# A hybrid decoder step: sample state update in the dense stage, gating inside the scan, state-input weighting on VectorE

## What is computed

```python
# prompt: chunks of 128 tokens, H = 32 heads of 64, G = 4 groups, state size N = 128
decay = exp(where(causal, la_cs[i] - la_cs[j], -inf))
y_diag = einsum('bcijgr,bcjgrp->bcigrp', (C @ B) * decay, xdt)
chunk_states = einsum('bcjgn,bcjgrp->bcgrpn', B, xdt * decay_to_end)
y = y_diag + (C @ h_prev) * exp(la_cs)
# sample: one token from a carried state, 8 sequences
hs = exp(dt * a) * h0 + B * (x * dt)          # the new state is an output
ys = einsum('bgn,bgrpn->bgrp', C, hs)
# both
yg = (y + d_skip * x) * silu(z)
yg = yg * rsqrt(mean(yg * yg over a group) + eps) * gnorm_w
out = yg @ w_out
```

## Time and profile before

| | us |
|---|---|
| three runs, median (lowest to highest) | 1814.99 (1813.65 to 1815.94) |
| the profiled execution, its own time | 1813.57 |
| its span in the trace | 1811.5 |
| scan, first state update to last y_out | 144.8 to 291.0 |
| gating and group norm | 291.0 to 334.3 |
| out-projection | 334.3 to 377.5 |
| norm | 377.5 to 397.6 |
| dense feed-forward stage | 397.6 to 590 |
| layer 1 and final norm, not touched by the change | 590 to 1811 |

### The profile page before, as it was taken

One profiled execution on the slowest core, in us unless ns is written; L12 is line 12 of the kernel. 1 busy time (PEld: TensorE's weight loads), 2 busy tenths in 40 slices (PEclk: granted clock), 3 DMA queues, 4 the chain that ended last, 5 costly groups with the idle time before them and its releaser, 6 DMA issues.

```text
span 1811.5 us, 26186 instructions
## 1 busy us (share of the span) xinstructions
PE 1676.7 (93%) x9438; PEld 1435.7 (79%) x9438; DVE 1350.5 (75%) x1733; ACT 1094.9 (60%) x1093; POOL 227.9 (13%) x140
## 2 busy tenths in 40 slices
PE   5898884879999899979999999999999999999995
PEld 4887773869999898958888888888888888888883
DVE  5797788544444676468979878889789888888985
ACT  5555555334443463347767777677777777777774
POOL 1002211025444222300000000000000000000000
PEclk9988787989999999979999999999999999999997
DMA  6345563356647544439999999999999999999995
GB/s 180 117 144 152 165 169 96 106 162 187 172 135 205 187 150 130 144 131 374 356 362 386 352 379 372 357 385 364 349 394 353 372 379 354 377 370 351 392 356 186
DMA packets 246213, 482.38 MB, mean 266 GB/s; under 512 B 10659, under 2 KB 151203, under 8 KB 245835
## 3 DMA queue, kind: packets, MB, share of 16 engines
q1 hardware_dynamic: 233152, 448.00, 70.0%
q0 software_dynamic: 7152, 26.03, 5.3%
q10 hardware_dynamic: 5838, 7.41, 1.2%
HBM read 463.80 MB, written 17.80 MB: 266 GB/s over the span
## 4 chain that ended last, share of the span: by engine, by line
PE 85%; DVE 8%; ACT 3%; DMA 2%; issue 1%; DVEq 0%; SPq 0%; ACTq 0%; POOLq 0%
PE bank L1296 12%; PE bank L1298 12%; PE bank L1297 12%; PE bank L938 8%; PE bank L939 8%; PE bank L940 8%; PE bank L1318 6%; PE bank L1317 6%; PE bank L1319 6%; PE bank L1270 1%; ACT part L377 1%; DVE part L389 1%; PE bank L1084 1%; DVE arena L1405 1%; DVE rs L1343 1%
## 5 line engine op out<-in xcount | busy, mean ns | idle before, releaser
L1896 DVE TENSOR_TENSOR raw_r<-raw_w,part 128x2048 fp32r<-128x2048 f32 x336 | 759.4, 2290 | 129.9 <-ACT part L851 119.0
L851 ACT ACTIVATE part<-raw_w 128x2048 fp32r<-128x2048 f32 x336 | 636.6, 1917 | 164.6 <-DMA raw_w<-in_moe_w_gu_dram 118.3
L1296 PE MATMUL bank<-part,xh 128*128 128x512 f32 x896 | 358.3, 400 | 1.5 <-DVE xl L1851 1.5
L1298 PE MATMUL bank<-part,xl 128*128 128x512 f32 x896 | 354.3, 395 | 0.0
L1297 PE MATMUL bank<-raw_r,xh 128*128 128x512 f32 x896 | 354.3, 395 | 0.0
L938 PE MATMUL bank<-ah,part 128*128 128x264 f32 x928 | 278.5, 300 | 11.4 <-DVE al L1356 8.0
L940 PE MATMUL bank<-al,part 128*128 128x264 f32 x928 | 269.2, 290 | 0.0
L1296 PEld LDWEIGHTS bank<-part,xh 128*128 128x128 f32 x896 | 168.4, 188 | 41.3 <-issue 1.9
L1298 PEld LDWEIGHTS bank<-part,xl 128*128 128x128 f32 x896 | 168.3, 188 | 41.2
L389 DVE TENSOR_TENSOR raw_r<-raw_w,part 128x1536 fp32r<-128x1536 f32 (+2 forms) x65 | 120.7, 1859 | 106.2 <-ACT part L377 105.7
L1297 PEld LDWEIGHTS bank<-raw_r,xh 128*128 128x128 f32 x896 | 168.6, 188 | 39.2
(11 more groups left out here) (361 smaller groups left out, 2315.5 us busy)
## 6 DMA issues: line engine op xcount, KB each, us to landing
raw_w<-in_moe_w_gu_dram SPq DMA_DIRECT2D x227, 1024.0 KB, 5.6
raw_w<-in_moe_w_down_dram SPq DMA_DIRECT2D x112, 1024.0 KB, 5.0
raw_w<-in_ffn_w_gu_dram SPq DMA_DIRECT2D x44, 512.0 KB, 5.3
raw_w<-in_ssd_w_in_dram SPq DMA_DIRECT2D x20, 1024.0 KB, 5.2
raw_w<-in_sgu_w_in_dram SPq DMA_DIRECT2D x16, 1024.0 KB, 5.6
raw_w<-in_ffn_w_down_dram SPq DMA_DIRECT2D x16, 704.0 KB, 4.9
raw_w<-in_state_ssm_dram POOLq DMA_DIRECT2D x16, 512.0 KB, 5.9
out_dram<-raw_w POOLq DMA_DIRECT2D x16, 512.0 KB, 3.9
```

What stands on the lines that cost most here:

```text
L851: act.activation(first_half(ND + n, 0, SLOT), raw_w[:, q, :], ACT.Copy).then_inc(S("part1"), 1)
L1296: mm(out, xh[:, k, :], w[0][:, kk, c], start=(k == 0), stop=False)
L1298: ins = mm(out, xl[:, k, :], w[0][:, kk, c], start=False, stop=(k == DT - 1))
L1896: tt(second_half(ND + n, 0, SLOT), raw_w[:, q, :], first_half(ND + n, 0, SLOT).bitcast(F32), ALU.subtract).then_inc(S("part2"), 1)
```

## The change

**The sample's state.** The scan no longer updates the state. Since C·(decay x h + B x) = decay x (C·h) + x (C·B), step t reads the old state (the eight products with C), multiplies the sums by the decay and adds a term that is prepared once, from C·B of each sequence (`cb`, formed in the in-projection at n = 12). The new states are formed in the dense feed-forward stage: the old ones are loaded a second time into three buffers (`old`), ACT decays four of the eight parts per weight tile (`decayed`), DVE adds the input (`updated`), GpSimd's queue stores. B and C are broadcast to the partitions by DMA, through a small buffer in DRAM (`bc_d`), instead of PE and ACT. The state loads of the scan go from GpSimd's queue to SP's, among the weight loads.

**The gate.** z stays in PSUM; ACT forms tanh(z/2), `z_out` on DVE forms (tanh + 1) z, `gated` multiplies by y, ACT squares and PE sums in the scan, two steps behind. Root, reciprocal and scaling of groups 0 and 1 are done at steps 10 to 15, those of groups 2 and 3 behind the scan. `out_first` multiplies k = 0 to 7 of m = 0 and of m = 1 first, then the rest of both.

**The decays.** `log_decay` is now six matmuls in reduced precision, and one of them adds the causal mask, so that the exponential can be taken straight from PSUM with a bias; `segments` is gone.

**The weighting** of the chunk states' inputs goes from GpSimd to DVE. `split_2` is all on DVE. The conv rows are transposed behind m = 2 to 7 of the out-projection (`conv_rows`) and copied by `conv_out`; the norm behind waits for their stores.

The core of the diff:

```diff
-            for n in range(15):
-                split_2(pool, n, True)
...
-            weighted(0)
             for t in range(IT):
...
+                pool.wait_ge(S("upd"), 2 * t + 2)
+                pool.dma_start(h_out[t], old[t % TB]).then_inc(S(f"new{t % TB}"), 16)
+                if t in (3, 7):
+                    spread(drive[:, (t // 4) % 2], 0, t // 4 + 2, f"drive{(t // 4) % 2}")
+                if t + TB < IT:
+                    pool.wait_ge(S(f"new{t % TB}"), 16 * (t // TB + 1))
+                    state_again(t + TB)
```

ScalarE in the scan:

```diff
+                    act.activation(ce[:, t % 2], psum[7][:, 0:256].rearrange("p (h i) -> p h i", h=2), ACT.Exp).then_inc(S("el_ready"), 1)
...
+                    for h in range(2):
+                        for c in range(2):
+                            act.activation(ex[t % 2][:, 2 * h + c, :], psum[2 + t % 2][:, 256 * h + P * c:256 * h + P * c + P],
+                                           ACT.Exp, bias=nla[:, c, 2 * t + h:2 * t + h + 1]).then_inc(S("ex_ready"), 1)
...
+                    act.activation(th, psum[(CT + t - 1) % 2][:, 0:T], ACT.Tanh, scale=0.5).then_inc(S("th_ready"), 1)
...
+                if t >= 2:
+                    square(t - 2)
+                if t % 2 == 1 and t < IT - 1:
+                    split_1(act, 15 + t // 2)
+                if t == 10:
+                    act.wait_ge(S("gms_ready"), 2)
+                    act.activation(rs[:, :, :], rs[:, :, :], ACT.Sqrt).then_inc(S("groot_ready"), 1)
```

VectorE in the scan, and the new functions:

```diff
+            def z_out(u):
+
+                dve.wait_ge(S("th_ready"), u + 1)
+                stt(out=zT[:, u, :], in0=th, scalar=1.0, in1=psum[(CT + u) % 2][:, 0:T],
+                    op0=ALU.add, op1=ALU.mult).then_inc(S("z_ready"), 1)
+
+            def gated(u):
+
+                dve.wait_ge(S("z_ready"), u + 1)
+                dve.wait_ge(S("y_done"), u + 1)
+                tt(zT[:, u, :], zT[:, u, :], xbc[:, u, :], ALU.mult).then_inc(S("gated"), 1)
...
+                if t < IT:
+                    own.settle()
+                    step(tt(ys, ys, sdec[:, t, :], ALU.mult))
+                    own.did(tt(xbc[:, t, NP_:T], xbc[:, t, NP_:T], ys, ALU.add))
+                    own.settle()
+                    dve.nop().then_inc(S("y_sample"), 1)
                 if t % 2 == 1 and t < IT - 1:
                     split_2(dve, 15 + t // 2)
...
+                if t % 4 == 2 and g + 1 < G:
+                    weighted(g + 1)
```

TensorE's log decays, and the wait ahead of the norm:

```diff
+                    pe.wait_ge(S("ex_ready"), 4 * t - 4)
+                if t:
+                    pe.wait_ge(S("el_ready"), t)
...
+                mm(out[:, :], identr[:, :], maskr[:, :].unsqueeze(1).to_broadcast((P, 4, P)), start=True, stop=False)
...
+            residual(1, ahead_out)
+            conv_out(5)
+            dve.wait_ge(S("conv_out"), 80)
             norm(1, IT)
```

More of the change, by code:

```diff
@@ L46 @@
 SB = 3
-HB = 4
+TB = 3
 EPS = 1e-5
@@ L561, in _ @@
+            for k in range(TB):
+                pool.wait_ge(S(f"new{k}"), 16 * len(range(k, IT, TB)))
             pool.wait_ge(S("v_out"), 16)
+            pool.iota(ioti[:, :], pattern=[[1, P]], base=0, channel_multiplier=0).then_inc(S("consts"), 1)
             def gather():
@@ L767, in ahead_down @@
                 split_1(act, D0 + 2 * m + 3)
+                if m < 6:
+                    decayed(2 * m + 20)
+                    decayed(2 * m + 21)
+                if m == 7:
+                    for k in range(TB):
+                        act.wait_ge(S(f"new{k}"), 16 * len(range(k, IT, TB)))
+                    act.dma_start(wsr, i["sgu_w_s"][0].rearrange("g i j -> i g j")).then_inc(S("late_in"), 16)
+                    for k in range(2):
+                        act.dma_start(bsr[8 * k:8 * k + 8, :], i["sgu_b_s"][0]).then_inc(S("late_in"), 16)
             norm(2, IT, ahead_down)
@@ L1090, in _ @@
[L1090 to L1106 removed]
+                if t >= 2:
+                    group_square(t - 2)
@@ new lines, in out_first @@
+            def out_first():
+                pe.wait_ge(S("z_ready"), IT)
+                both = [None, None]
+                for m in range(2):
+                    both[m] = weight(20 + m)
+                    for k in range(8):
+                        pe.wait_ge(S("yg2"), k + 1)
+                        product(psum[m][:, 0:T], [u[:, k, :] for u in both[m]], (zh[:, k, :], zl[:, k, :]), k == 0, False)
+                    if m == 0:
+                        group_square(IT - 1)
+                for k in range(8, IT):
+                    pe.wait_ge(S("yg2"), k + 1)
+                    for m in range(2):
+                        ins = product(psum[m][:, 0:T], [u[:, k, :] for u in both[m]], (zh[:, k, :], zl[:, k, :]), False, k == IT - 1)
+                        if k == IT - 1:
+                            ins.then_inc(S("o_mm"), 1)
@@ L1114, in out_proj @@
                         pe.wait_ge(S("x_ready"), xbase + m - 1)
-                    for c in range(per):
+                    for c in range(per if n > 1 or m >= 2 else 0):
                         w = weight(n0 + per * m + c)
```

586 lines of the change are left out of this document (316 added, 270 removed).

## The result

The changed kernel takes 1786.87 us (median of four runs, 1781.87 to 1791.52) against 1815.3 for the kernel before, a ratio of 0.984 with an interval of 0.981 to 0.988. It is faster by 28 us. The forecast was 1771 with a range of 1752 to 1794: the sign and the range hold, the size doesn't; 44 us were expected. It is one of the slower runs of the changed kernel, which spread over 10 us; the four of the kernel before beside them spread over 2, those beside the experiments over 5 to 6.

What follows compares the result with a forecast made beforehand. The scan was taken as a loop through VectorE and ScalarE, with TensorE following. Gains 24 (scan), 31 (behind it) and 1.5, less 5.4, 5.4 and 2, gave 43.7 off 1813.6; with 1.4 for the median, 1771 us, range 1752 to 1794.

Steps and rivals of the forecast that it cites:

- T: End of the scan, at the last y_out: forecast 267 us against 291.0 before, 24 us gained, ends 255 and 280.
- The conv transposes: Out-projection, behind tiles m = 2 to 7: six groups at 0.9 us with hand-over, 5.4 us lost on TensorE.
- rival B: Dense feed-forward stage: state transfers delay the weights by 10 to 20 us, total 1779 to 1789; chance 0.10.
- Layer 1: Later stages: VectorE's splits alone in the memory without GpSimd's share, 1.5 us gained, bounds 0 to 3.
- rival A: Scan: the two loops interlock, hardly shortening it; 8.9 to 9.6 us a step, T 280 to 291, total 1784 to 1795; chance 0.16.
- wrong if steps stay near 9 us: Scan: sign that would refute the prediction, which expected 6.18 us a step and pairs of 12.4 on VectorE.
- loop start: Scan: loop begins near 137 us, after half a split, C·B product, sample prelude, split 14 and weighting 0 on VectorE.
- steps 0 and 1: Scan: backlog of splits and states, 9.1 us each, 18.2 together.
- steps 2 to 10, with the clock's allowance and the root: Scan: nine steps of 6.18 us plus two chunk states of 2.5, 60.6; 6 for the clock, 3 for the root.
- steps 11 to the end: Scan: five steps of 6.2 us plus reciprocal, scalings and second parts, 40.9, and 1.5 for the loop's end.
- TensorE's and ScalarE's loop: Scan: log_decay (0.7), y matmuls, z tile, a group sum, split_1, exponential and hand-overs; 12.2 us per pair of steps.
- rival D: Scan: broken work leaves TensorE at 1.2 GHz throughout, 11.5 us a step, T = 321, total 1825, slower; chance 0.06.

Runs made afterwards that it cites:

- experiment 7: Changed kernel with the wait for the stores of the last 1024 conv columns moved from ahead of the norm to behind it; 1785.30 us, ratio 0.984.
- experiment 1: Changed kernel with the scan's weight splits moved from the end of odd steps to the end of the next even step; 1771.41 us, ratio 0.977.
- experiment 2: Changed kernel with root and first parts one step later, behind the exponentials, and the mean square ahead of the weighting; 1768.90 us, ratio 0.974.
- experiment 4: Changed kernel with both the later weight splits and the moved normalization (root, first parts, mean square); 1757.28 us, ratio 0.968.
- experiment 8: Changed kernel with splits, normalization and conv-store wait moved, and mean squares at steps 6 and 10 ahead of y_out; 1750.74 us, ratio 0.966.
- experiment 3: Changed kernel with 14 unused matmuls of 248 columns added on TensorE behind the z tile of odd steps from 3 on; 1787.41 us, ratio 0.985.
- experiment 5: Changed kernel with the weighting of the chunk states' inputs back on GpSimd instead of VectorE; 1775.80 us, ratio 0.980.
- experiment 10: The kernel of experiment 8 with the weighting on GpSimd instead of VectorE; 1745.94 us, ratio 0.963.

## Why the prediction was right in sign and wrong in size

**What held.** Behind the scan: tile 2 begins at T + 18.0, or T + 18.7 from the last y_out, by which the prediction counts; 18 were forecast. The conv transposes lost 39.4 - 36.9 = 2.5 us on TensorE up to the end of m = 7, 5.4 were charged, and the norm lost 19.2 - 15.1 = 4.1 instead of 5.4; the DMA wait in it was 2.94 us against 3.0, and experiment 7 shows that 1.8 of them count. The residual of m = 1, by which the prediction put it, is not the mark: it stands at 315.85, as a split is ahead of it on VectorE, while TensorE goes on at 312.2. Dense stage: 203.6 against 203.5, so rival B did not come; the 2 us charged were not needed. The Trainium skill ("DMA: Bandwidth & Descriptors", section "Issuing engines are not separate DMA queues") has the transfers of all issuing engines interleave on the same 16 DMA engines. The trace agrees in that the weights' transfers landed later (8.4 us against 5.3 for a gate and up half), and the effect on the time was nothing, since they still landed ahead of need. Layer 1: 1.8 us gained, 1.5 estimated; no run shows whether for the reason given. The table loads at step 10 took 1.28 us each, as in the earlier trace rows, and from the end of the root to the next exponential are 1.31 us.

**What was luck.** The time lies above the forecast's own 1759 to 1784 and inside rival A's 1784 to 1795, to which 0.16 was given; the range holds it because it takes in A. The scan ended 27 us late, and some 6 came back because the norm, the conv transposes and the dense stage cost less than charged. The sign rests on the gain behind the scan.

**The step that failed is T**, 294.2 instead of 267: rival A's length in its place, and 3 us beyond its end. By the prediction's own sign ("wrong if steps stay near 9 us") its scan was wrong: steps 2 to 10 took 9.06 us on average, and pairs of them 15.9 to 20.2 instead of 12.4. Rival A had the loops interlock through y_out, settling and the bank of exponentials; experiments 1, 2 and 4 show that it was the splits, the first parts and the mean squares queued ahead of what releases TensorE. The working has T in four terms:

| term | forecast | measured | off by |
|---|---|---|---|
| loop start | 137 | 139.1 | + 2.1 |
| steps 0 and 1 | 18.2 | 17.3 | - 0.9 |
| steps 2 to 10, with the clock's allowance and the root | 60.6 + 6 + 3 | 81.5 | + 11.9 |
| steps 11 to the end | 40.9 + 1.5 | 56.3 | + 13.9 |

The 2.1 us at the loop start can't be told from chance: with the same code ahead of the loop it began at 139.1, 140.7 and 144.4. Two slips of the sums matter little: the seven terms of a step add up to 5.03, not 5.05, and half a pair of before is 8.97, not 9.1.

*Steps 2 to 10.* The shortest pair, 8 and 9, with the chunk states, took 15.87 us at a clock of 0.94 where 12.35 + 2.5 was summed. TensorE's and ScalarE's loop was sized 1 us too short per pair: log_decay takes 1.05 to 1.17 us at the full clock, not 0.7. Over the nine steps that makes 4.5, the mean squares 3.8 (see below); the 3.6 that are left are by this estimate the clock, beyond the 6 charged. The 6 were taken without a reason from a range that ended at 17; with the same waits the same code ran 8.5 us apart by its clock, and between the changed kernel and experiment 8 the same work differs by 21 us. Against rival D the prediction has TensorE's waits for y_out shrink. They did, but others took their place (29.3 us of waiting before, 32.1 after): VectorE and ScalarE were relieved, but the order in which they release TensorE was not. With another order the sum comes out: in experiment 8 steps 2 to 10 took 60.4 us and those behind 38.2, against the 60.6 and 42.4 of the working. So the work was sized well, and the order was not in the sum.

*Steps 11 on.* The normalization was summed as VectorE's work (3.6 + 8 x 0.43 + 8 x 0.36) with 3 for the root ahead of it. The work was right and the place was not: first parts stand ahead of the next exponential on ScalarE, and behind a split and the reciprocal on VectorE. A sum over one engine does not see a chain through three; experiment 2 moved the root, the first parts and the mean squares, and took out 12.6 us of waiting (3.8 of them the mean squares'), experiment 4 with the splits 20.2.

*The weighting.* It was charged as hidden under TensorE's chunk states. In fact the mean square was queued behind it on VectorE, and TensorE's next group sum behind that: 2.27 and 1.50 us, which the working does not have. The working asks what is queued behind an added wait, but not what is queued behind added work.

Rival D did not come: the scan's mean clock was 0.82, not 0.50. What sets how far it falls in one execution and not in the next stays open; the runs show only that less waiting goes with a higher clock (32 us of waits: 0.82 to 0.87; 27 to 18: 0.83 to 0.86; 12 to 9: 0.90 to 0.96), and that experiment 3, which put work into some of the gaps, does not settle whether the gaps are the cause.

## What to carry to other kernels

Relieving the fullest engine of a loop pays only as far as the next one allows: sum the loop for every engine, and where two come out alike, follow the order by which they release each other instead of taking the larger sum. In an in-order list the place of an instruction can cost more than the instruction: what releases the bound engine (here the exponentials) goes first, and long work that nobody waits for (splits, first parts) behind it. Where a change has several parts, run each alone; here one (the weighting) cost time, and one (normalization inside the scan) gained nothing until it was put in another place.

## What the runs showed of the hardware

The granted clock differs between executions of the same code, and with it the time: three scans with 32 us of waiting each had 0.82, 0.84 and 0.87 and took 155.1, 152.0 and 146.6 us. DMA engines shown busy at 0.99 of a stage still took 8.4 MB more in it, at 290 instead of 264 GB/s, for 5.8 us. A weighting of 3 x 512 columns took 1.9 us on VectorE. On GpSimd it took 3.0 to 3.5 us in experiment 5 and 5.3 and 5.6 beside the busier VectorE of experiment 10, and beside it a VectorE product of 512 columns went from 0.68 to 1.53 us.
